# Two 64-feature products in place of each 128-feature product in the compression of keys and values

## The reference, cut to what matters

```python
def compress_blocks(t, pos, w1, w2):
    ...
    blocks = jnp.concatenate([sub[:, :, r:r + n_cmp] for r in range(ratio)], axis=3)
    blocks = (blocks + pos).reshape(B, H, n_cmp, CMP_BLOCK * dh)
    return jax.nn.gelu(blocks @ w1) @ w2

kc = rmsnorm_2(compress_blocks(heads(kc), cmp_pos[0], cmp_w1[0], cmp_w2[0]), k_norm[0])
vc = compress_blocks(heads(vc), cmp_pos[1], cmp_w1[1], cmp_w2[1])
```

## Time and profile before

| | |
|---|---|
| median of 3 runs | 1682.28 us (1681.22 to 1685.14) |
| the profiled execution | 1686.05 us, span 1684.2 us |
| PE busy | 1652.2 us (98%) |
| DVE busy | 1095.1 us (65%) |
| ACT busy | 919.5 us (55%) |
| chain that ended last | PE 86%, DVE 6%, ACT 5% |
| mean granted TensorE clock | 0.993 |

### The profile page before, as it was taken

The page is one execution under the profiler, slowest core; times in us unless marked ns, Lnnn a source line. Parts: engine busy times, 40 slices in busy tenths (PEclk is TensorE's granted clock), DMA queues, the critical chain, the costliest instruction groups (busy, mean ns, idle before and its releaser), DMA issues.

```text
span 1684.2 us, 30435 instructions
## 1 busy us (share of the span) xinstructions
PE 1652.2 (98%) x13180; PEld 1566.1 (93%) x13180; DVE 1095.1 (65%) x1371; ACT 919.5 (55%) x1248; POOL 159.2 (9%) x63
## 2 busy tenths in 40 slices
PE   7999999999999999999999899999999999999999
PEld 7999989999999989998988699998999898799998
DVE  6888868664666567756578856656655667665554
ACT  6966778445444455434487844444443447754432
POOL 0000000000022101220000002210122000012210
PEclk9999999999999999999899899999999999999999
DMA  7555344454455455545542235545554564245543
GB/s 268 184 176 172 130 150 143 184 179 147 150 190 186 156 197 199 200 162 172 195 143 101 101 126 192 183 155 197 203 198 160 173 220 151 101 143 184 191 155 129
DMA packets 44629, 284.01 MB, mean 169 GB/s; under 512 B 4944, under 2 KB 6608, under 8 KB 17744
## 3 DMA queue, kind: packets, MB, share of 16 engines
q1 hardware_dynamic: 44352, 281.99, 48.0%
q10 hardware_dynamic: 144, 0.08, 0.0%
HBM read 281.00 MB, written 1.05 MB: 167 GB/s over the span
## 4 chain that ended last, share of the span: by engine, by line
PE 86%; DVE 6%; ACT 5%; issue 2%; DMA 1%; DVEq 0%; ACTq 0%
PE bank L509 85%; ACT WH L1152 2%; DVE WL L1737 2%; PE bank L660 1%; DVE HT L1793 0%; ACT SB L1275 0%; ACT XM L1159 0%; DVE XM L1745 0%; ACT XR L1159 0%; ACT FB L1176 0%; DVE FB L1763 0%; DVE STAT L1882 0%; DMA RAW<-in_nsa_w_out 0%; DMA PAR<-in_par 0%; DVE FA L2178 0%
## 5 line engine op out<-in xcount | busy, mean ns | idle before, releaser
L1737 DVE TENSOR_TENSOR WL<-RAW,WH 128x2048 fp32r<-128x2048 f32 (+1 forms) x282 | 590.3, 2096 | 272.2 <-ACT WH L1152 272.0
L509 PE MATMUL bank<-XR,WH 128*128 128x256 f32 x3648 | 651.2, 282 | 11.2 <-DVE WL L1924 10.7
L1152 ACT ACTIVATE WH<-RAW 128x2048 fp32r<-128x2048 f32 (+1 forms) x282 | 493.1, 1752 | 217.4 <-PE bank L509 211.2
L509 PEld LDWEIGHTS bank<-XR,WH 128*128 128x128 f32 x3648 | 559.7, 189 | 15.5 <-DVE WL L1924 10.7
L509 PE MATMUL bank<-XR,WL 128*128 128x256 f32 x1824 | 511.1, 280 | 0.0
L509 PEld LDWEIGHTS bank<-XR,WL 128*128 128x128 f32 x1824 | 344.4, 189 | 0.0
L509 PE MATMUL bank<-XF,WH 128*128 128x512 f32 x880 | 305.3, 392 | 0.0
L509 PE MATMUL bank<-XM,WH 128*128 128x256 f32 x1664 | 299.0, 282 | 3.3 <-DVE XM L1745 1.8
L509 PEld LDWEIGHTS bank<-XM,WH 128*128 128x128 f32 x1664 | 256.9, 190 | 4.8 <-DVE XM L1745 2.8
L509 PE MATMUL bank<-XF,WL 128*128 128x256 f32 x880 | 246.0, 280 | 0.0
L509 PE MATMUL bank<-XM,WL 128*128 128x256 f32 x832 | 234.2, 281 | 0.0
(11 more groups left out here) (278 smaller groups left out, 1667.0 us busy)
## 6 DMA issues: line engine op xcount, KB each, us to landing
RAW<-in_f1i SPq DMA_DIRECT2D x44, 1024.0 KB, 4.9
RAW<-in_f2i SPq DMA_DIRECT2D x44, 1024.0 KB, 4.9
RAW<-in_w_in SPq DMA_DIRECT2D x35, 1024.0 KB, 4.9
RAW<-in_w_ffn_in SPq DMA_DIRECT2D x22, 1024.0 KB, 4.8
RAW<-in_f1o SPq DMA_DIRECT2D x32, 704.0 KB, 4.1
RAW<-in_f2o SPq DMA_DIRECT2D x32, 704.0 KB, 4.1
RAW<-in_diff_w_in SPq DMA_DIRECT2D x12, 1024.0 KB, 5.0
RAW<-in_w_ffn_out SPq DMA_DIRECT2D x16, 704.0 KB, 4.2
```

The source lines that it names most:

```text
L509: return e.matmul(o, l, r, start=start, stop=stop)
L1152: e.activation(split_at(u, cols)[0], RAW[:, u % NRAW, 0:cols], ACT.Copy).then_inc(hi_done.tick(u), 1)
L1737: e.tensor_tensor(lo, RAW[:, u % NRAW, 0:cols], hi.bitcast(f32), sub).then_inc(lo_done.tick(u), 1)
```

## The change

Each product of `compress` with 128 stationary columns becomes two with 64, z = 0 and 1, whose results go to partitions 0 to 63 and 64 to 127 of the same bank at the same columns. Both read the same 60 moving columns. In `compressed_values` the four copies g are split in the same way, two for each z. What each element of the bank holds is the same as before, and so are the semaphores, the banks and the transfers.

```diff
@@ compress
-                        t = mm(b[:, c * 64:c * 64 + 60], w[:, i8, c * 128:c * 128 + 128], BLK[:, ii * 60:ii * 60 + 60],
-                               ii == 0 and c == 0, ii == 15 and c == 1)
+                        for z in range(2):
+                            at = c * 128 + z * 64
+                            t = mm(b[z * 64:z * 64 + 64, c * 64:c * 64 + 60], w[:, i8, at:at + 64], BLK[:, ii * 60:ii * 60 + 60],
+                                   ii == 0 and c == 0, ii == 15 and c == 1)
@@ compressed_values
-                        t = mm(b[:, hk * 64:hk * 64 + 64], HR[:, kt, hk].rearrange("p g n -> p (g n)"), W2[:, 1, kt, :], kt == 0, kt == 1)
+                        for z in range(2):
+                            t = mm(b[z * 64:z * 64 + 64, hk * 64:hk * 64 + 64], HR[:, kt, hk, 2 * z:2 * z + 2].rearrange("p g n -> p (g n)"),
+                                   W2[:, 1, kt, :], kt == 0, kt == 1)
```

## The result

| | before | after |
|---|---|---|
| median (13 runs each) | 1682.28 us (1678.92 to 1686.32) | 1677.98 us (1672.97 to 1682.56) |
| ratio, 95% interval | | 0.9971 (0.9959 to 0.9983) |
| profiled execution: span | 1684.2 us | 1671.9 us |
| its NSA loop, from the first `compress` record to the transposes at p = 18 | 69.05 us | 64.38 us |

The kernel is 4.3 us faster by the medians; 5.2 were forecast. The two profiled spans differ by more, 12.3 us. Of that 4.67 us lie inside the loop. The loop also begins 2.0 us earlier, and the code behind it takes 5.6 us less, though both are unchanged. Part of that goes with the granted clock: outside the loop the lower level lasts 16.0 us in the profile before and 9.5 us in the one after. A single pair of profiles must therefore be compared stage by stage, and the times by the runs.

The account below looks back on a forecast made before the run. TensorE (PE) was taken as the bound on average, with waits between engines deciding what passes; 1.5 + 0.72 + 0.72 + 0.92 + 1.3 = 5.2 us off the median 1682.3 gave 1677.1 us, range 1674.3 to 1682.3.

Parts of the forecast that it names:

- The size of the saving on PE: Products of `compress` and `compressed_values`: 31.4 ns a record, 2.0 us a call; PE relieved of 7.6 us altogether.
- (a): Split products: the halves don't overlap, 106 ns a record, time 1697 us; chance 5%.
- (b): Split products: no gain from accumulation in place, or loads one behind the other; 55 ns a record, 1682 us; chance 10%.
- p = 6: Behind `compress(0, 1)`: PE 3.1 us earlier, VectorE only 1.5 + 0.72 = 2.2, its own work being the cover.
- p = 7: `compress(1, 0)` ends 4.7 us earlier; ScalarE's wait for `nsa_w_out` shrinks to about half a microsecond; VectorE gains 0.72, 2.9 earlier.
- p = 8: PE, up to 4.8 us earlier, waits about 0.8 us for bank 3 at the last query part's projection; no effect.
- p = 9 and 10: PE waits near 2 us ahead of `compressed_keys`; VectorE gains its 0.92 us wait in full and is 3.9 earlier.
- p = 10 to 12: VectorE's unbroken work carries the advance of 3.9 us on.
- p = 12 and 13: `compressed_values` gives 1.3 us, within VectorE's 1.95 us of waits for PE; the advance becomes 5.2.
- rival (d): Low clock stretch at 943 to 950 goes away as `compressed_values` moves; 7.4 us gained, 1675 us; chance 10%.
- The sum: Over the NSA loop, 5.2 us of PE's 7.6 come through; the other 2.4 become waits of PE.
- Rival (c): Clock falls behind new PE waits at 916.6 to 921.5; about 2.3 us of gain left, 1680 us; chance 17%.

Follow-up runs that it names:

- values only: Kernel before with only `compressed_values` split in halves, `compress` left at full width; median 1679.34 us, ratio 0.9985.
- two products a call: Kernel before with 14 of the 16 full-width products of each `compress` call left out, waits and transfers kept; median 1677.15 us, ratio 0.9979.
- the first products alone: Kernel before with only `compress` split in halves, `compressed_values` left at full width; median 1683.05 us, ratio 1.0002.
- the unread products: Changed kernel plus seven fp32 products, results overwritten, ahead of PE's waits in p = 9 to 11; 1674.90 us, ratio 0.9958. Also added to other kernels.

## Why the prediction was right

The time lies 0.9 us from the forecast, and the mechanism up to p = 10 is the one that was forecast, with every step a little short. Behind that the sum came near by offsets that were not foreseen, which is partly luck. By its steps:

- **The size of the saving on PE.** 31.4 ns a record and 2.0 us a call: measured 2.01 us. Results that accumulate in place cost nothing that shows. Rivals (a) and (b) are out. Case (a) did not fit the rows of before either: load and streaming one behind the other would make 110 + 51 = 161 ns a record at full width, where 110 were read. The Trainium skill's rule in "TensorE: Matmul & The Clock Gate", Part 3, that loads are pulled ahead only when the row group differs, doesn't hold for these products: with the same rows and other columns, in turn, a record costs 31 ns, in a row 52 ns, and with quarters 14 ns. The charge of about 60 cycles that the Trainium skill's "TensorEngine Tiling (Array Packing)", Instruction Overhead, puts on each matmul would be 25 ns at 2.4 GHz as an estimate; a quarter-width product, which is two records, takes 28.4 ns, so these runs speak against such a charge only if it is meant for each record.
- **p = 6:** VectorE 1.5 earlier; measured, against its scaling at p = 5 (892.35 and 890.21), (899.25 - 896.01) - 2.14 = 1.10. Here the step failed in part: the sum of squares at 893.96 waited 0.23 us for ScalarE's square, and 0.1 us went in front of the call. I also overlooked that the transposes behind it need the bank that ScalarE's L1236 frees (0.36 us of wait at 897.74). PE starts the second call, counted from the first, only 0.34 us earlier instead of 1.5.
- **p = 7:** 2.2 forecast, 1.84 measured; the 0.72 was gained in full, since VectorE was the cover. `compress(1, 0)` ended not 4.7 but 3.3 earlier, so the transfer was issued later than I had it and ScalarE still waited 1.51 us instead of half a microsecond. It was hidden, and the 0.72 at L1737 was gained: 2.9 forecast, 2.63 measured.
- **p = 8:** the forecast wait of 0.8 us for bank 3 did not come; PE was less early than I had it. Nothing hung on it.
- **p = 9 and 10:** 3.9 forecast, 3.64 measured. The wait ahead of `compressed_keys` was 0.96 instead of 2 us, for PE was less early; that of the sum of squares was 0.60 instead of 0.4.
- **p = 10 to 12:** here the step failed in a small part. VectorE's work was not unbroken: at 930.58 it waited 0.24 us for ScalarE's rounding of the next weights, so the advance was (936.04 - 930.58) - 2.14 = 3.32 there and not 3.9.
- **p = 12 and 13:** `compressed_values` gave 0.88 instead of 1.3 in the profiled execution, 1.90 us at the low level, near my upper bound of 2.0; with the clock at full level it gave 1.70 (values only). Yet the advance grew by 4.56 - 3.32 = 1.24, nearly the 1.3, because the clock came back at 940.7: the three pieces behind `compressed_values`, from scores to transposes, took 942.61 - 939.59 = 3.02 us, and 949.63 - 945.10 = 4.53 before. That is the 1.5 us which rival (d) had named, and it stood in for the forecast gain of the products. Before, these pieces were all at the lower level:

```profile
946.68 1.55 PE L509 MATMUL bank<-PT,FA 128*64 128x256 f32 x8
948.16 1.54 PE L660 MATMUL bank<-CON,FB 128*128 128x128 f32 x6
949.63 1.27 PE L509 MATMUL bank<-FB,FA 64*128 64x15 f32 x16
```

  The advance at VectorE's L2296 is (950.93 - 944.23) - 2.14 = 4.56 where 5.2 was forecast, and 4.57 at the end of the loop: the transfers did not hold it up.
- **The sum.** 4.6 us in the profile's loop, 4.3 by the medians, 4.0 at equal clock, with the reservations made there. The interval of the ratio, 2.9 to 6.9 us of gain, holds the forecast. That a relief of PE beyond the halves gives nothing up to `compressed_values` is shown by the kernel with two products a call; for the whole time it is not.
- **The clock.** Rival (c) put the trouble at the wrong place: the clock didn't fall at p = 9, where it was looked for. It fell at the same piece as before, the small products of p = 11, but stayed low for 10.2 us there instead of 3.4, and ahead of `compressed_values` the advance was down to 48.63 - 46.04 = 2.6 us, where the three other kernels with the same first products and the same work on VectorE have 3.3 to 3.4 (they start it at 45.20, 45.23 and 45.30). That the two halves of the change go with opposite shifts of the mean clock (0.9901 with the first products alone, 0.9942 with the values alone) was not in the prediction at all; had only the first products been changed, I would have forecast 3.9 us of gain and found none.

What stays open: why the kernel with the first products alone has so low a clock. The stretch behind p = 11 is at the low level in its profile and the 12 runs agree, but that it is the full-width `compressed_values` that keeps it there was only inferred, from the two halves and from the way the 13 profiles sort; the unread products were placed ahead of it, and no run put them behind it.

## What to carry to other kernels

Plain fp32 products with 60 moving columns took 110 ns a record here, more than twice the 51 ns estimated for their streaming, so the load of their 128 weight columns was what to attack; splitting the columns in two halves that write to different partitions, and issuing them strictly in turn, made 64 products 44% shorter without any other change. A saving on the busiest engine is worth what passes each wait behind it: follow it from wait to wait, including the PSUM banks that a late engine has to free, and check it with a kernel that leaves the work out. And less work can go with a lower clock, as with the first products alone (0.9901, against 0.9927 for before on the same chip): compare the granted clock over many runs, with before measured beside them, before a small difference is put down to the edit.

## What the runs showed that was not expected

- Half-width records in a row cost 52 ns, in turn 31.4 ns, and quarter-width ones in turn 14.2 ns.
- The run-to-run spread of this kernel (1676.5 to 1689.2 us over 35 runs of before) follows the mean granted clock, 0.988 to 0.996, at 1.2 us for 0.001.
- With seven products that nobody reads, 2.2 us of work in PE's waits, the mean clock is 0.9961 where the changed kernel's is 0.9934, and the mean time is 2.2 us lower, on other chips.
- From the start of `compressed_values` to the loop's end, the six profiles with its full-width products take 20.4 us or more, the seven with halves 19.0 us or less.
- With 128 records in a call, TensorE once stood still for 1.91 us without a wait that the profile shows.
